# Experts' down weights: two neighbouring rows per partition, and transposes that read every second column

## The chip, the cores and the metric

The kernel runs on one core of a Trainium2 chip. The metric is the device time of one execution in microseconds (us), and what is compared is the median of several executions. The profile is one further execution, recorded by the hardware profiler.

A core has TensorE (PE in the rows; PEld is its load of the stationary operand), VectorE (DVE), ScalarE (ACT), GpSimd (POOL) and SyncE (SP), which here issues nearly all the transfers. Work buffers lie in SBUF on 128 partitions, the results of matrix products in the eight PSUM banks. Each product has a stationary operand, loaded by an LDWEIGHTS, and a moving one that streams past it. Transfers run on 16 DMA engines.

## The reference, cut to what matters

Two blocks follow one another on a sequence of 256 rows of width 1024, all in float32. The part that the change touches is the mixture of experts at the end of the first block: eight experts of inner width 3584, two of which are chosen for each row.

```python
def swiglu(h, w_gate, w_up, w_down):
    return (jax.nn.silu(h @ w_gate) * (h @ w_up)) @ w_down

def moe_swiglu(h, w_router, w_gate, w_up, w_down):
    ...
    for e in range(N_EXPERTS):
        y = swiglu(h, w_gate[e], w_up[e], w_down[e])
        out = out + gates[..., e:e + 1].astype(h.dtype) * y
    return out
```

`w_gate` and `w_up` are 1024x3584 for each expert, `w_down` is 3584x1024, so an expert has 42 MiB of weights and all eight have 336 MiB. Each row of `w_down` is 1024 float32, 4096 bytes in one run in HBM, and row r + 1 follows row r directly.

## The kernel before

Ahead of the experts come a gated linear attention, a dense feed-forward layer, an attention and the router; behind them a second block with its own mixers and feed-forward layer. The experts take the stretch from about 457 to 1440 us of the span.

**Pieces.** All weights come as pieces of 1 MiB, 2048 float32 on each of 128 partitions. For one expert, the inner width is cut into seven slices j of 512 (`EJ`). Each slice has six pieces: two of gate and two of up (`"g"`, `"u"`: 512 of the 1024 input rows by 512 columns, four rows on a partition in runs of 2048 bytes), and two of down (`"d"`: 256 of the 512 rows by all 1024 columns). The list `uorder` sets the order: gate and up of slice j, then down of slice j - 1. That makes 42 pieces for an expert (`UC`) and 336 for all eight, 112 of them down.

**Stations of a piece.** SP loads it (`load_expert`, L610 to 628) into one of six raw slots (`NRX`; four in `raw`, two in the arena, which is why rows name both). ACT writes a rounded copy of it (`wh`, L1027), DVE the difference between the piece and that copy (`wl`, L1543). PE then makes three products for each exact one (L1980 to 1982: both high parts, and each low part with the other's high part). There are four slots for `wh` and `wl` (`NW`). ACT waits for the transfer and for PE to be done with the piece four earlier; SP waits for DVE to be done with the piece six earlier.

**What PE does.** For each expert the rows that chose it are gathered by products with a one-hot matrix (L2299), 128 at a time. Then for each slice j: gate, then the transposes of slice j - 1 (`transposed`, L2327 to 2332), then up, then down of slice j - 1 (`down`; in the last slice `last_down`). Gate, up and down are 12 products a piece, 128x512 each. The activation `eact`, 128 rows by 512 inner columns in the arena, is transposed in four blocks of 128 columns into bank 4; ACT and DVE split the transposed blocks in two parts (`eactTh`, L1059; `eactTl`, L1622), and these are the stationary operands of down. Block k of the transposed activation, with inner columns on partitions, meets the rows of `w_down` that lie on the same partitions: block k in 0 and 1 goes with the first down piece, in 2 and 3 with the second.

**Which rows lie where.** The helper `kpn` puts rows k * 128 + p of a down piece at place k of partition p: each partition gets two runs of 4096 bytes that lie 512 KiB apart in HBM. So block k of the transposes is the 128 neighbouring columns from k * 128. In `T.transpose(out, in_, ident)` the data is the stationary operand and the identity the moving one; rows name the moving one first.

Each engine runs its own instructions in the order of the program text; nothing is scheduled by a planner here.

Of the kernel before, what the change touches and what calls it, by code (L numbers as in the profile page):

```python
# [16 lines left out]
def build(nc, IN, out):  # L17
# [6 lines left out]
    P = 128  # L24
    _, S, D = IN["x"].shape
# [35 lines left out]
    with ctx:  # L61
        def sb(name, shape, dt=F32):
            return ctx.enter_context(nc.sbuf_tensor(name, shape, dt))
# [3 lines left out]
        def sg(name):  # L67
            if name not in sems:
                sems[name] = ctx.enter_context(nc.semaphore(name))
            return sems[name]  # L70
# [18 lines left out]
        ident = sb("ident", [P, P])  # L89
# [22 lines left out]
        bank = [ctx.enter_context(nc.psum_tensor(f"bank{b}", [P, 512], F32)) for b in range(8)]  # L112
# [6 lines left out]
        def ar(n):  # L119
            a = arena[:, ar_at[0]:ar_at[0] + n]  # L120
            ar_at[0] += n
            assert ar_at[0] <= AR, ar_at[0]
            return a
# [194 lines left out]
        def kpn(ap):  # L318
            return ap.rearrange("(k p) n -> p k n", p=P)
# [141 lines left out]
        def moe_raw(c):  # L461

            s = c % NRX
            return (raw[:, (M0 + s) % NR, :] if s < NR else extra[:, s - NR, :]), raw_moe[s]
# [72 lines left out]
        eact = ar(2 * EJ).rearrange("p (a n) -> p a n", a=2)  # L537
# [65 lines left out]
        def _(sp):  # L603
# [11 lines left out]
            def load_expert(c, e):  # L615

                kind, j, k = uorder[c % UC]
                ee = e + c // UC
                to, arrived = moe_raw(c)
                if kind == "d":  # L620
                    r0 = j * EJ + k * (EJ // 2)
                    src = IN["moe_w_down"][0].rearrange("e f n -> (e f) n")[bass.ds(ee * FE + r0, EJ // 2), :]
                    src = kpn(src)
                else:
                    src = IN["moe_w_gate" if kind == "g" else "moe_w_up"][0, bass.ds(ee, 1), k * (D // 2):(k + 1) * (D // 2),
                                                                          j * EJ:(j + 1) * EJ]
                    src = src.rearrange("a (k p) n -> p (a k) n", p=P)
                sp.dma_start(to.rearrange("p (k n) -> p k n", k=src.shape[1]), src).then_inc(arrived, 16)
# [33 lines left out]
            for c in range(NR):  # L662
                split_done(sp, N_PRE - NR + c)
                load_expert(c, 0)
            for hp in range(SH // 2):
                see(sp, ("so", hp))
            for c in range(NR, NRX):
                load_expert(c, 0)
            sp.wait_ge(sg("more_ready"), 1)
            more = sp.value_load(more_i[0:1, 0:1], min_val=0, max_val=NPAIR)  # L670
            with sp.Fori(0, more + (NPAIR - 1)) as p:
                e = (p % NPAIR) * 2
                for c in range(NRX, PC):
                    moe_split(sp, lambda a, b: p * a + b, c - NRX)
                    load_expert(c, e)
                e2 = ((p + 1) % NPAIR) * 2
                for c in range(NRX):
                    moe_split(sp, lambda a, b: p * a + b, c + PC - NRX)
                    load_expert(c, e2)
# [1250 lines left out]
        def _(pe):  # L1930
            T = nc.tensor
# [170 lines left out]
            for k in range(KD):  # L2102
                ins = T.matmul(ps[0:GR, 0:S], wglr[:, k, :], xT[:, k, :], start=(k == 0), stop=(k == KD - 1))  # L2103
# [4 lines left out]
            for b in range(2):  # L2108
                ps = take(("gate", b))
                for j in range(2):  # L2110
                    hd = 2 * b + j
                    ins = T.matmul(ps[:, j * S:(j + 1) * S], wgu[:, hd * P:(hd + 1) * P], glrT, start=True, stop=True)
# [7 lines left out]
            for st in range(2):  # L2120
# [4 lines left out]
                for hd in range(GH):  # L2125
                    o = hd * S + st * P
                    ins = T.matmul(ps[0:GC, hd * P + GC:(hd + 1) * P], g["ke"][:, hd, st, :], g["qd"][:, o + GC:o + P],
                                   start=True, stop=True)
# [3 lines left out]
            for hd in range(GH):  # L2132
                o = hd * S
                ins = T.matmul(ps[:, hd * P:(hd + 1) * P], g["E"][:, o:o + P], g["B"][:, o + P:o + S], start=True, stop=True)
# [27 lines left out]
            for k in range(3):  # L2162
                n = V_ROWS[k]
# [87 lines left out]
            for hp in range(SH // 2):  # L2251
                ps = take(("so", hp))
                for i in range(2):
# [5 lines left out]
                    ins = T.matmul(ps[:, i * S + P:(i + 1) * S], sv[:, 1, vs], sU[:, hd, S:384], start=False, stop=True)  # L2259
# [50 lines left out]
            def experts(at, more_follow):  # L2310
# [5 lines left out]
                for i in range(2):  # L2316
# [10 lines left out]
                    def transposed(j):  # L2327
                        n = NEJ * i + j
                        pe.wait_ge(sg("moe_act"), at(2 * NEJ, n + 3))
                        for k in range(4):  # L2330
                            ins = T.transpose(bank[4][:, k * P:(k + 1) * P], eact[:, n % 2, k * P:(k + 1) * P], ident[:, :])  # L2331
                        ins.then_inc(sg("moe_Tfull"), 1)

                    def down(j, between=None):
# [37 lines left out]
                    for j in range(NEJ):  # L2372
                        n = NEJ * i + j
                        pe.wait_ge(sg("moe_act"), at(2 * NEJ, n + 1))
                        gate_up(bank[n % 2], "g", j)
                        if j == 1:
                            pe.wait_ge(sg("moe_h"), at(8, 4 * i + 1))
                        if j:
                            transposed(j - 1)
                        gate_up(bank[2 + n % 2], "u", j)  # L2380
                        if j == NEJ - 1:
                            down(j - 1, lambda: transposed(NEJ - 1))
                        elif j:
                            down(j - 1)
                        if j == 3:
                            pe.wait_ge(sg("moe_gates"), at(2, i + 1))
                            for t in range(TT):
                                T.transpose(bank[7][:, t * P:(t + 1) * P], oh[:, t, :], ident[:, :])
                            for t in range(TT):
                                ins = T.matmul(bank[7][:, S:S + 1], oh[:, t, :], gnow[:, t:t + 1], start=(t == 0), stop=(t == TT - 1))  # L2390
                            ins.then_inc(sg("moe_ohfull"), 1)
# [36 lines left out]
            for t in range(TT):  # L2428
                for k in range(KD):
                    ins = T.matmul(ps[:, 16 * t:16 * t + 16], xT[:, k, t * P:(t + 1) * P], ws[:, k, :],  # L2430
                                   start=(k == 0), stop=(k == KD - 1))
# [103 lines left out]
            for a, row in enumerate((mS, iF)):  # L2535
                for t in range(TT):
                    ins = T.transpose(ps[:, (TT * a + t) * P:(TT * a + t + 1) * P], row[:, t * P:(t + 1) * P], ident[:, :])
# [65 lines left out]
```

## Time and profile before

| what | value |
|---|---|
| median of 3 runs | 1820.54 us |
| lowest and highest | 1818.07 and 1821.10 us |
| the profiled execution, its own time | 1818.59 us |
| its span in the profile | 1816.9 us |
| PE busy | 1783.6 us (98%) |
| PEld, DVE, ACT, POOL busy | 85%, 77%, 62%, 6% |
[...]
| data moved | 479.27 MB in 244356 packets |

The profiled execution took 1818.59 us, of which 1816.9 are the span that the rows divide; 1.7 us lie around it. It is 1.95 us below the median of the three other runs. A busy PE says only that some product is under way: products are pipelined, one of 128x512 lasts some 390 ns from its start to its modelled end, but the next one starts earlier than that. The distance from start to start is therefore what a product costs.

### The profile page before, as it was taken

Reading aid. Unit: us, or ns where it says so; the run is one execution under the profiler, and the core shown is the slowest. Engines: PE = TensorE matmul, PEld = TensorE weight load, DVE = VectorE, ACT = ScalarE, POOL = GpSimd, SP = SyncE. Lnnn points to the kernel's source line nnn. Section 1 sums busy time; section 2 is a strip of 40 time slices with the busy share of each in tenths; the row PEclk is TensorE's granted clock in tenths of the full one; section 3 lists DMA queues with packets and bytes.
Section 4 is the critical chain, followed back from the end, with each engine's and each line's share of the span. In section 5 each row is a group of like instructions: output and inputs, shape, how many; then the busy total and the mean of one; then the engine's idle time right before and its main releaser. Section 6 shows DMA issues by size and latency. Waiting matters only on the chain.

```text
span 1816.9 us, 25802 instructions
## 1 busy us (share of the span) xinstructions
PE 1783.6 (98%) x10010; PEld 1542.8 (85%) x10010; DVE 1404.5 (77%) x1164; ACT 1131.6 (62%) x942; POOL 115.1 (6%) x133
## 2 busy tenths in 40 slices
PE   7999999999999999999999999999999999999999
PEld 6779999998888888888888888888888788789998
DVE  6565455656888988989889889888888879767775
ACT  6344344463677777776777767777767745745553
POOL 7000000000000000000000000000000008500000
PEclk9999999999999999999999999999999999999999
DMA  7445565542899998998998989989989944325561
GB/s 237 163 141 182 189 199 171 171 155 71 323 381 347 353 373 317 387 370 323 378 371 328 371 318 388 364 321 383 372 324 373 319 134 136 120 82 185 175 206 49
DMA packets 244356, 479.27 MB, mean 264 GB/s; under 512 B 11759, under 2 KB 80137, under 8 KB 244249
## 3 DMA queue, kind: packets, MB, share of 16 engines
q1 hardware_dynamic: 243385, 476.43, 73.3%
q8 instruction: 80, 1.31, 0.3%
q10 hardware_dynamic: 864, 1.31, 0.2%
q14 instruction: 27, 0.22, 0.0%
HBM read 476.66 MB, written 1.05 MB: 263 GB/s over the span
## 4 chain that ended last, share of the span: by engine, by line
PE 89%; DVE 7%; ACT 1%; issue 1%; DMA 0%; POOL 0%; DVEq 0%; ACTq 0%; SPq 0%; POOLq 0%
PE bank L1980 27%; PE bank L1982 27%; PE bank L1981 27%; DVE wl L438 2%; PE bank L2299 1%; PE bank L2331 1%; DVE xT L1296 1%; DVE xTl L1239 1%; PE bank L2368 0%; PE bank L1949 0%; PE bank L2369 0%; DVE h L1309 0%; DVE xn L1252 0%; PE bank L2103 0%; ACT xn L854 0%
## 5 line engine op out<-in xcount | busy, mean ns | idle before, releaser
L1980 PE MATMUL bank<-wh,xTh 128*128 128x512 f32 x1568 | 620.7, 396 | 4.3 <-DVE wl L438 2.8
L1982 PE MATMUL bank<-wh,xTl 128*128 128x512 f32 x1568 | 612.0, 390 | 0.0
L1981 PE MATMUL bank<-wl,xTh 128*128 128x512 f32 x1568 | 611.2, 390 | 0.0
L1543 DVE TENSOR_TENSOR wl<-raw,wh 128x2048 fp32r<-128x2048 f32 x224 | 512.2, 2291 | 92.6 <-ACT wh L1027 90.9
L1027 ACT ACTIVATE wh<-raw 128x2048 fp32r<-128x2048 f32 x224 | 429.2, 1918 | 120.7 <-PE bank L1982 120.7
L1980 PEld LDWEIGHTS bank<-wh,xTh 128*128 128x128 f32 x1568 | 295.2, 188 | 66.5 <-DVE wl L438 3.7
L1982 PEld LDWEIGHTS bank<-wh,xTl 128*128 128x128 f32 x1568 | 294.8, 188 | 62.7
L1981 PEld LDWEIGHTS bank<-wl,xTh 128*128 128x128 f32 x1568 | 295.3, 188 | 58.5
L438 DVE TENSOR_TENSOR wl<-raw,wh 128x2048 fp32r<-128x2048 f32 x112 | 254.7, 2292 | 68.3 <-ACT wh L431 66.5
L1980 PE MATMUL bank<-xTh,wh 128*128 128x256 f32 x1024 | 290.8, 284 | 1.2 <-DVE xTl L1239 0.8
L1981 PE MATMUL bank<-xTl,wh 128*128 128x256 f32 x1024 | 289.8, 283 | 0.0
L1982 PE MATMUL bank<-xTh,wl 128*128 128x256 f32 x1024 | 289.8, 283 | 0.0
L1543 DVE TENSOR_TENSOR wl<-arena,wh 128x2048 fp32r<-128x2048 f32 x112 | 255.6, 2286 | 0.4 <-ACT wh L1027 0.2
L1027 ACT ACTIVATE wh<-arena 128x2048 fp32r<-128x2048 f32 x112 | 215.3, 1922 | 52.0 <-PE bank L1982 52.0
L431 ACT ACTIVATE wh<-raw 128x2048 fp32r<-128x2048 f32 x116 | 219.5, 1912 | 39.4 <-PE bank L1982 32.5
L1980 PEld LDWEIGHTS bank<-xTh,wh 128*128 128x128 f32 x1024 | 196.4, 192 | 3.7 <-DVE xTl L1239 1.6
L1981 PEld LDWEIGHTS bank<-xTl,wh 128*128 128x128 f32 x1024 | 196.5, 192 | 0.7
L1982 PEld LDWEIGHTS bank<-xTh,wl 128*128 128x128 f32 x1024 | 196.4, 192 | 0.0
L1980 PE MATMUL bank<-wh,acth 128*128 128x512 f32 x192 | 75.3, 392 | 0.3 <-DVE actl L1493 0.3
L1981 PE MATMUL bank<-wl,acth 128*128 128x512 f32 x192 | 75.0, 390 | 0.0
L1982 PE MATMUL bank<-wh,actl 128*128 128x512 f32 x192 | 74.7, 389 | 0.0
L713 POOL TENSOR_TENSOR rstd<-ms,cst 128x4 f32<-128x4 f32 (+1 forms) x4 | 3.5, 865 | 1051.0 <-DVE ms L1683 1009.7
(379 smaller groups left out, 1384.6 us busy)
## 6 DMA issues: line engine op xcount, KB each, us to landing
raw<-in_moe_w_up SPq DMA_DIRECT2D x112, 1024.0 KB, 7.7
arena<-in_moe_w_gate SPq DMA_DIRECT2D x96, 1024.0 KB, 7.4
raw<-in_moe_w_down SPq DMA_DIRECT2D x96, 1024.0 KB, 7.2
raw<-in_w_up SPq DMA_DIRECT2D x22, 1024.0 KB, 5.5
raw<-in_moe_w_gate SPq DMA_DIRECT2D x16, 1024.0 KB, 7.5
arena<-in_moe_w_down SPq DMA_DIRECT2D x16, 1024.0 KB, 7.4
raw<-in_gla_w_in SPq DMA_DIRECT2D x12, 1024.0 KB, 7.8
raw<-in_w_in SPq DMA_DIRECT2D x12, 1024.0 KB, 6.3
```

The lines of the kernel that those rows point to most:

```text
L431: nc.scalar.activation(wh[:, i % NW, :], raw[:, i % NR, :], ACT.Copy).then_inc(hi_ready[ph], 1)
L438: V.tensor_tensor(wl[:, i % NW, :], raw[:, i % NR, :], wh[:, i % NW, :].bitcast(F32), ALU.subtract).then_inc(lo_of[i][0], 1)
L713: G(V.tensor_tensor(rstd[:, c0:c0 + n], ms[:, c0:c0 + n], c_half[:, 0:n], ALU.pow), "rstd_ready")
L1027: V.activation(wh[:, s, :], src, ACT.Copy).then_inc(sg("hi_moe"), 1)
L1239: C(V.tensor_tensor(hi_lo[1][ix], src[ix], hi_lo[0][ix].bitcast(F32), ALU.subtract), "xl_ready")
L1296: ins = V.tensor_tensor(dst[:, 4 * half:4 * half + 4, t * P:(t + 1) * P], ps, gains.unsqueeze(2).to_broadcast([P, 4, P]), ALU.mult)
L1543: V.tensor_tensor(wl[:, s, :], moe_raw(c)[0], wh[:, s, :].bitcast(F32), ALU.subtract).then_inc(lo_moe, 1)
L1980: T.matmul(o, xh, yh, start=first, stop=False)
L1981: T.matmul(o, xh, yl, start=False, stop=False)
L1982: return T.matmul(o, xl, yh, start=False, stop=last)
L2299: ins = T.matmul(b[:, k * P:(k + 1) * P], xn[:, t, kk * P:(kk + 1) * P], oh[:, t, :], start=(t == 0), stop=(t == TT - 1))
L2331: ins = T.transpose(bank[4][:, k * P:(k + 1) * P], eact[:, n % 2, k * P:(k + 1) * P], ident[:, :])
```

## The change

Two places change together. The transfer of a down piece puts rows 2p and 2p + 1 of the piece on partition p, so each partition gets one run of 8192 bytes and the whole piece is 1 MiB without a gap. The transposes take the columns to match: within each half of 256 columns, one block takes the even columns and the next the odd ones, so the stationary operand is read with a step of two elements (8 bytes). Sizes, counts, buffers, waits and the order of the work are as before. Every sum over inner columns has the same terms in another order.

```diff
@@ -620,7 +620,7 @@
                 if kind == "d":
                     r0 = j * EJ + k * (EJ // 2)
                     src = IN["moe_w_down"][0].rearrange("e f n -> (e f) n")[bass.ds(ee * FE + r0, EJ // 2), :]
-                    src = kpn(src)
+                    src = src.rearrange("(p k) n -> p k n", p=P)
                 else:
@@ -2328,7 +2328,8 @@
                         pe.wait_ge(sg("moe_act"), at(2 * NEJ, n + 3))
                         for k in range(4):
-                            ins = T.transpose(bank[4][:, k * P:(k + 1) * P], eact[:, n % 2, k * P:(k + 1) * P], ident[:, :])
+                            rows_of = eact[:, n % 2, k // 2 * S:(k // 2 + 1) * S].rearrange("p (f two) -> p two f", two=2)
+                            ins = T.transpose(bank[4][:, k * P:(k + 1) * P], rows_of[:, k % 2, :], ident[:, :])
```

No instruction is added, removed or moved on any engine. On SP's queue only the shape of the down transfers differs. Before, behind an up piece and ahead of the gate pieces of the next slice:

```order
L628 DMA raw<-in_moe_w_down 128x2x1024
L459 REGISTER_ALU
L628 ISA
L628 DMA raw<-in_moe_w_down 128x2x1024
L459 REGISTER_ALU
```

And in the changed kernel, at the same place:

```order
L628 DMA raw<-in_moe_w_down 128x2048
L459 REGISTER_ALU
L628 ISA
L628 DMA raw<-in_moe_w_down 128x2048
L459 REGISTER_ALU
```

Both are 1 MiB; the two runs of 1024 elements have become one of 2048.

## Rows read from the trace of the kernel before

**Rows 1.** Page: busy shares, clock by slices, packets, chain that ended last.

```profile
PE 1783.6 (98%) x10010; PEld 1542.8 (85%) x10010; DVE 1404.5 (77%) x1164; ACT 1131.6 (62%) x942; POOL 115.1 (6%) x133
...
PEclk9999999999999999999999999999999999999999
...
DMA packets 244356, 479.27 MB, mean 264 GB/s; under 512 B 11759, under 2 KB 80137, under 8 KB 244249
...
PE 89%; DVE 7%; ACT 1%; issue 1%; DMA 0%; POOL 0%; DVEq 0%; ACTq 0%; SPq 0%; POOLq 0%
```

**Rows 2.** Windows: busy us of PE, PEld, DVE, ACT, POOL; clock, DMA share, GB/s.

```profile
174.30:179.70 5.40, 5.40 (x26) 4.48 (x25) 5.07 (x5) 2.55 (x2) 0.00 (x0) 1.00 0.14 21
902.00:917.40 15.40, 15.40 (x69) 12.74 (x68) 13.86 (x12) 11.85 (x8) 0.00 (x0) 1.00 1.03 378
600.00:1400.00 800.00, 800.00 (x3729) 664.12 (x3728) 708.44 (x443) 585.76 (x399) 0.00 (x0) 1.00 0.97 358
```

**Rows 3.** Waits of PE, 460 to 1445 us: who, for whom, total, times, longest.

```profile
PE bank L1980 <- DVE xTl L1590: 0.7, 1, 0.7
```

**Rows 4.** Line L2331, the transposes: durations ns min/median/max.

```profile
L2331 PEld LDWEIGHTS bank<-ident,arena x224: 139/141/143, 477.9 to 1439.1; 128*128 128x128 f32 x112
L2331 PE MATMUL bank<-ident,arena x224: 270/272/273, 478.2 to 1439.2; 128*128 128x128 f32 x112
```

**Rows 5.** Chain around a group of transposes: start, us on the chain.

```profile
901.02 0.44 PE bank L2331 x4
```

**Rows 6.** Timeline of PE in the experts, slice of 900 to 918 us.

```profile
900.86 0.60 PE L2331 MATMUL bank<-ident,arena 128*128 128x128 f32 x4
901.21 0.47 PE L1980 MATMUL bank<-wh,xTh 128*128 128x512 f32 x1
901.52 0.39 PE L1981 MATMUL bank<-wl,xTh 128*128 128x512 f32 x1
...
917.64 0.60 PE L2331 MATMUL bank<-ident,arena 128*128 128x128 f32 x4
```

**Rows 7.** ACT, exponentials over pieces of a tile: the line, and its first instruction.

```profile
L865 ACT ACTIVATE arena<-arena x8: 417/418/447, 1499.1 to 1553.3; 128x256 f32<-128x256 f32 x8
...
1499.09 0.45 ACT L865 ACTIVATE arena<-arena 128x256 f32<-128x256 f32 x1 [0.18 <-DVE arena L1750]
```

**Rows 8.** Timeline of DVE, products of tiles: step of two, then runs of two, four.

```profile
1501.30 1.09 DVE L1322 TENSOR_TENSOR arena<-arena 128x256 f32<-128x256 f32 x1
1511.05 0.42 DVE L1322 TENSOR_TENSOR arena<-arena 128x256 f32<-128x256 f32 x1
1515.84 0.97 DVE L1322 TENSOR_TENSOR arena<-arena 128x256 f32<-128x256 f32 x1
```

**Rows 9.** DMA view: transfers by source, KB each, median us from issue to landing.

```profile
raw<-in_moe_w_up SPq DMA_DIRECT2D x112, 1024.0 KB, 7.7
...
raw<-in_moe_w_down SPq DMA_DIRECT2D x96, 1024.0 KB, 7.2
...
raw<-in_ffn_w_gate SPq DMA_DIRECT2D x11, 1024.0 KB, 5.4
...
raw<-in_ffn_w_down SPq DMA_DIRECT2D x11, 1024.0 KB, 5.0
```

**Rows 10.** The down transfers of the experts: us from issue to landing.

```profile
DMA to landing us min/median/max: 4.8/7.2/9.3
```

**Rows 11.** Timelines of SP and ACT: a down piece issued, and read.

```profile
902.76 0.37 SPq L628 DMA_DIRECT2D raw<-in_moe_w_down  x1
...
915.12 1.92 ACT L1027 ACTIVATE wh<-raw 128x2048 fp32r<-128x2048 f32 x1 [0.80 <-PE bank L1982]
```

**Rows 12.** Timeline of PE in the feed-forward layer: two products, 22 steps apart.

```profile
174.51 0.40 PE L1981 MATMUL bank<-wl,acth 128*128 128x512 f32 x1
...
179.51 0.39 PE L1982 MATMUL bank<-wh,actl 128*128 128x512 f32 x1
```

**Rows 13.** Waits of SP's queue, whole run: for whom, total, times, longest.

```profile
SPq L628 <- DVE wl L1543: 779.0, 328, 7.2
```

## The prediction, made blind

> **What bounds the kernel now.** I read the page first, then the windows, then PE's own waits. On the page PE is busy for 98% of the span, its clock row stands at full speed in every slice, and the chain that ended last lies on PE for 89% and on DMA for 0% [rows 1]. In the windows (the three are feed-forward down products, one slice of the experts, and most of the experts) the experts are denser than that: between 600 and 1400 us PE is busy for 800.00 of 800.00 us at a granted clock of 1.00, while the DMA share is 0.97 at 358 GB/s [rows 2]. Both look full, so the waits must tell which one sets the pace. In the whole stretch of the experts PE waited 0.7 us, once, for DVE [rows 3]; no wait of PE or ACT there ends on a DMA. SP, by contrast, stood 779.0 us in 328 waits for DVE to give back a slot [rows 13]. The transfers follow the compute, and PE's instruction stream sets the end.
>
> So a change counts here if it changes what PE's own instructions cost, or if it makes a transfer so late that its slack is used up.
>
> **Part one, the transfers.** 112 down pieces of 1 MiB change from two runs of 4096 bytes per partition to one of 8192. Follow one piece. SP issues it at 902.76, and ACT, whose sixth copy since the freed slot's it is, reads it at 915.12, held back by PE and not by the transfer [rows 11]. That is 12.36 us from issue to use. The down transfers take 7.2 us in the median and 9.3 at most [rows 10]: 5.2 us of slack, 3.1 in the worst case. This slack, ahead of ACT's copy, is the cover.
>
> How does run length act on landing? Up pieces with runs of 2048 bytes land in 7.7 us, down pieces with runs of 4096 in 7.2; in the feed-forward layer gate pieces with runs of 1024 take 5.4 and down pieces with 4096 take 5.0 [rows 9]. Longer runs gain 0.4 to 0.5 us, in other places of the queue, too. I expect 7.2 to fall by 0 to 0.5 us. Since nothing waits for it, the saving only makes SP's pieces lie ready earlier. I cost it at nothing; an increase would be nothing too until it reaches 3.1 us in the worst piece.
>
> Could lighter transfers speed up PE itself, through less traffic into the buffers that PE reads? The trace has the comparison. In the feed-forward layer, at a DMA share of 0.14 and 21 GB/s [rows 2], 22 steps from product to product take 179.51 - 174.51 = 5.00 us, 0.2273 each [rows 12]. In the experts, at 1.03 and 378 GB/s [rows 2], the 72 products of one slice lie between 901.21 and the next transposes at 917.64; the 71 steps from 901.52 take 16.12 us, 0.2270 each [rows 6]. With eighteen times the traffic a product costs the same. I take 0.
>
> **Part two, the transposes.** There are 8 experts x 7 slices x 4 = 224, all of whose stationary loads now step by two. A group starts at 900.86, the next product at 901.21, and the one after that at 901.52, where the usual step would be 0.227: the group costs 0.35 + 0.31 - 0.227 = 0.433 us [rows 6], and the chain gives 0.44 [rows 5]. Four transposes, 0.109 each; 56 groups make 24.5 us of PE time. Nothing hides that time: what a transpose gains or loses is gained or lost at the end of the kernel. The load is part of it, and its 139 to 143 ns [rows 4] are longer than the 109 ns between transposes, so loads and transposes run into one another with no gap to spare.
>
> The trace of before shows no TensorE load with a step. I bound it from both sides.
> - Below: 0. The step doesn't change the number of elements or instructions, and no row shows a strided read that is faster than a plain one; a gain is excluded on that ground.
> - Nearest row above: ScalarE's exponentials read and write 256 float32 in pieces of a tile. In the first one the pieces are single elements with a step of two, in the later ones runs of 2 to 128. The first took 447 ns, the median is 418 [rows 7]. That is 29 ns for 256 elements with both sides strided; for 128 elements 14.5 ns, times 224: 3.2 us.
> - Far row: VectorE's product of tiles took 1.09 us with a step of two, 0.42 with runs of two, but 0.97 with runs of four [rows 8]. An instruction without the step is as slow, so most of it is something else, and I give no weight to the factor of 2.6. Taken at its word it is 1.6 x 24.5 = 39 us.
>
> I take 0, the lower end: the closest row loses 7% with a strided read and a strided write together, the load has only the read, and that instruction was the first of its kind, so part of its 29 ns may be start-up. Both ends stay for the range.
>
> On strided reads the row above shows +29 ns. [...] Nothing in this trace shows where TensorE's own limit lies.
>
> What stands behind the transposes: the first down product of a slice comes a whole up stage later, some 5.4 us (24 products x 0.227), and needs ACT's and DVE's parts of bank 4. A few tenths more on the transposes would be hidden there. Only PE's own time counts.
>
> **The sum.** Profiled execution 1818.6 us + transfers 0 + PE's steps 0 + transposes 0 = 1818.6. That execution lies 1.95 us below the median of the three runs, so the forecast for the median is **1820.5 us**, with its own range 1817 to 1824.
>
> **Rivals.**
> - **The strided load takes twice as long.** Mechanism: a load that takes every second element gets half as many useful elements from each read of the buffer. Place: the 224 stationary loads. Price: 0.109 us more for each, 24.5 us, giving 1845 us. It decides from 16 ns per transpose (3.6 us in all). For it: loads and transposes are back to back, nothing covers them, and ScalarE's row is not zero. Against it: at +7% ScalarE is far from double. A mild form, 16 to 30 ns per transpose, gives 1824 to 1827.
> - **Longer runs relieve PE.** If the products of the experts (336 pieces x 12 = 4032) each got 1 ns shorter, 4.0 us would be gained: 1816.5 us. For it: DMA share 0.97. Against it: 0.2273 and 0.2270 us a step at 21 and at 378 GB/s.
> - **The transfers become the bound.** A slice takes 917.64 - 900.86 = 16.78 us [rows 6] for six pieces, 2.80 each. If each down piece occupied the engines 2.8 us longer, the slice would grow by up to 5.6 us, and 56 slices by 313. It decides when landing rises from 7.2 beyond 12.4 us. For it: there is little idle DMA time. Against it: the direction of the landing times above.
> - **The change does nothing.** If the 8192 bytes are cut into two packets of 4096, the packet count stays at 244356 [rows 1] and the time is that of the forecast.
>
> **How the numbers follow.** A measurement of this kernel tells about 0.2%, 3.6 us, from no change. Forecast (the rival that does nothing included) 0.75; PE relieved 0.06; mild penalty 0.06; doubled load 0.11; transfers as the bound 0.02. The range has to hold the forecast's 1817 to 1824, and reaches down to 1816.5 less half a microsecond and up to the mild penalty's 1827: 1816 to 1827 leaves out the last two, 0.13. Faster 0.06, same 0.75, slower 0.19.
>
> **What would show it.** The line of the transposes should keep its loads near 141 ns and its matmuls near 272, and a group should stand on the chain with 0.44 us; a doubled load shows as about 0.87. The steps of the 128x512 products should stay at 0.227. The packets should fall by 112 x 128 = 14336 if each run is one packet. Down pieces should land in 6.7 to 7.2 us, SP should still wait for DVE, and PE for no transfer. The prediction is wrong if the group has grown beyond 0.50 us (16 ns x 4), or if a wait that ends on a DMA appears in the experts.

## The result, and the profile after

The changed kernel took 1822.99 us in the median of 18 runs (1821.42 to 1826.3), the kernel before 1820.40 (1814.96 to 1823.34). The ratio is 1.0021, with a 95% interval of 1.0014 to 1.0027: a small slowdown, 2.5 to 4.9 us, clear of noise. The profiled execution took 1822.76 us; its span is 1821.0 at a mean granted clock of 0.997, against 1816.9 at 0.998 before.

First the page, where little has moved. The packets fell by 14336 (230020 from the 244356 of [rows 1]), exactly 112 x 128, so each run of 8192 bytes is one packet, and the down pieces land sooner: 7.0 us in the median and 8.5 at most, from 7.2 and 9.3 [rows 10].

```profile
span 1821.0 us, 25802 instructions
...
DMA packets 230020, 479.27 MB, mean 263 GB/s; under 512 B 11759, under 2 KB 80137, under 8 KB 215577
...
PE 89%; DVE 7%; ACT 1%; issue 1%; DMA 0%; POOL 0%; DVEq 0%; ACTq 0%; SPq 0%; POOLq 0%
```

```profile
DMA to landing us min/median/max: 4.7/7.0/8.5
```

The line of the transposes (now L2332) is where the change shows; it answers to [rows 4]. The columns are minimum, median and maximum in ns.

```profile
L2332 PEld LDWEIGHTS bank<-ident,arena x224: 194/199/205, 477.6 to 1441.6; 128*128 128x128 f32 x112
L2332 PE MATMUL bank<-ident,arena x224: 271/280/282, 477.8 to 1441.7; 128*128 128x128 f32 x112
```

A load with a step of two lasts 199 ns in the median instead of 141, a transpose 280 instead of 272. The chain gives a group 0.46 us, where [rows 5] has 0.44, and PE's timeline shows the same slice as [rows 6], from one group to the next:

```profile
901.75 0.62 PE L2332 MATMUL bank<-ident,arena 128*128 128x128 f32 x4
902.13 0.47 PE L1980 MATMUL bank<-wh,xTh 128*128 128x512 f32 x1
902.44 0.39 PE L1981 MATMUL bank<-wl,xTh 128*128 128x512 f32 x1
...
918.59 0.62 PE L2332 MATMUL bank<-ident,arena 128*128 128x128 f32 x4
```

From group to group it is 918.59 - 901.75 = 16.84 us, where it was 917.64 - 900.86 = 16.78. One such pair is at the limit of the timeline's two decimals, so I took the mean over the 32 slices of a run that have 72 products and nothing else between two groups (24 in `same_delay`, which changes eight of them). In the four kernels with plain single transposes there (before, `load_only`, `permute_on_dve`, `same_delay`) it agrees within 0.001 us:

| kernel | last product to group | group to next product | next but one to the twelfth, each | slice |
|---|---|---|---|---|
| before | 0.231 | 0.353 | 0.2289 | 16.787 |
| after | 0.240 | 0.380 | 0.2308 | 16.840 |

Further behind, a product's step is 0.2267 in both. So a slice grew by 0.053 us: 0.009 ahead of the group, 0.027 in it, and some 0.02 over the ten products behind it. 56 groups make 3.0 us, 13.3 ns for each of the 224 transposes. The experts as a whole, from the first group to the last, grew from 960.67 to 963.54 us, by 2.9.

The spans of the two profiled executions differ by 4.1 us. Of that 2.9 lie in the experts, -0.4 ahead of them, and 1.6 behind, where the program did not change. There the windows show TensorE's granted clock, at the place where the second block begins (columns as in [rows 2]); first the changed kernel, then the kernel before at the same place in the program:

```profile
1474.50:1477.90 3.40, 3.40 (x30) 3.32 (x29) 1.06 (x3) 2.76 (x2) 0.00 (x0) 0.97 1.10 369
1477.90:1481.30 3.40, 3.40 (x16) 3.40 (x17) 0.86 (x5) 0.95 (x1) 1.16 (x1) 0.50 0.46 142
1481.30:1484.70 3.40, 3.40 (x18) 3.40 (x18) 0.00 (x0) 0.00 (x0) 0.00 (x0) 0.53 0.00 0
```

```profile
1475.40:1478.80 3.40, 3.40 (x30) 3.40 (x31) 0.86 (x5) 0.89 (x1) 1.17 (x1) 1.00 0.44 136
```

In the changed kernel's profile the clock stood at 0.50 of full for nearly 7 us, from 1477.7 to 1484.5, and PE got through 16 to 18 products in 3.4 us where it otherwise does 30. Counted product by product, it lost 3.0 us there against the kernel before. The timeline shows what PE did as it fell, 32 products of only 16 columns:

```profile
1474.88 4.30 PE L2431 MATMUL bank<-ws,xT 128*128 128x16 f32 x32
```

In the profile of before, the clock stood at 1.00 there, behind the same 32 products. In that profile it fell later, from 1590.5 to 1597.3 us. The changed kernel's clock fell a second time at nearly that place, for half as long. First the kernel before, then the changed one:

```profile
1590.50:1597.30 6.80, 6.33 (x18) 5.26 (x19) 5.67 (x17) 4.00 (x6) 0.00 (x0) 0.50 0.01 2
```

```profile
1597.10:1600.50 3.40, 3.40 (x11) 2.73 (x11) 2.99 (x13) 2.56 (x4) 0.00 (x0) 0.51 0.02 5
```

In the profile of `load_only`, below, the clock stayed up at both places, and against it the two stretches of these rows cost 3.0 and 1.6 us. So the 1.6 us behind the experts are 3.0 lost at 1480 less 1.4 that the changed kernel lost less at 1600. That the clock can fall at these places is no property of the change: the experiments have it without the step and without the new transfers (0.50 from 1499.4 us in `twice_plain`, from 1594.1 in `same_delay`).

### The profile page after: what moved, and what is told of

Same layout as the page of the kernel before. It is cut to its first block, busy times and chain, and to the rows that moved or that the text cites. A ratio compares the mean times of both kernels' runs of the same rounds, so it can differ in the third digit from the quotient of the medians.

```text
span 1821.0 us, 25802 instructions
## 1 busy us (share of the span) xinstructions
PE 1788.1 (98%) x10010; PEld 1549.8 (85%) x10010; DVE 1404.5 (77%) x1164; ACT 1131.7 (62%) x942; POOL 114.8 (6%) x133
## 2 busy tenths in 40 slices
DMA packets 230020, 479.27 MB, mean 263 GB/s; under 512 B 11759, under 2 KB 80137, under 8 KB 215577
## 4 chain that ended last, share of the span: by engine, by line
PE 89%; DVE 7%; ACT 1%; issue 1%; DMA 0%; POOL 0%; DVEq 0%; ACTq 0%; SPq 0%; POOLq 0%
PE bank L1980 27%; PE bank L1982 27%; PE bank L1981 27%; DVE wl L438 2%; PE bank L2299 1%; PE bank L2332 1%; DVE xT L1296 1%; DVE xTl L1239 1%; PE bank L2369 0%; PE bank L1949 0%; PE bank L2370 0%; DVE h L1309 0%; DVE xn L1252 0%; PE bank L2103 0%; ACT xn L854 0%
```

## The experiments

Three questions were open. Is it the transfers or the step that costs? Does the tail belong to it? And what does a strided operand cost TensorE, in a load that stands bare, in one that is hidden, and on the moving side?

**Transfers alone.** `load_only` is the kernel before with the first half of the diff.

```diff
-                    src = kpn(src)
+                    src = src.rearrange("(p k) n -> p k n", p=P)
```

> The kernel before with only the transfers changed (8192 bytes in one run per partition); the transposes read neighbouring columns as before, so the down products pair activations with the wrong rows of the weights, and the output is not the reference's. Theory of the step (the 224 stationary loads with a step of two cost 13 to 14 ns each, 0.054 us a group): nothing is left here, slice of the experts 16.79 us as before, ratio 0.999 to 1.001. Rival, the transfers' new shape costs the time (by buffer traffic beside PE): slice 16.84 us, ratio 1.0015 to 1.003.

Measured: 1818.07 us against 1818.74, ratio 0.9994 (0.9985 to 1.0003); the mean slice is 16.787 us. The timeline has 900.64 to 917.42:

```profile
900.64 0.60 PE L2331 MATMUL bank<-ident,arena 128*128 128x128 f32 x4
...
917.42 0.60 PE L2331 MATMUL bank<-ident,arena 128*128 128x128 f32 x4
```

The new transfers cost nothing and bring nothing (16.787 us a slice with both).

**The step alone.** `step2_only` is the second half of the diff, with the old transfers.

```diff
-    ins = T.transpose(bank[4][:, k * P:(k + 1) * P], eact[:, n % 2, k * P:(k + 1) * P], ident[:, :])
+    rows_of = eact[:, n % 2, k // 2 * S:(k // 2 + 1) * S].rearrange("p (f two) -> p two f", two=2)
+    ins = T.transpose(bank[4][:, k * P:(k + 1) * P], rows_of[:, k % 2, :], ident[:, :])
```

> The kernel before with only the transposes changed (step of two), the transfers as before; again activations meet the wrong rows, so the output is not the reference's. Theory of the step: slice 16.84 us, loads of the transposes near 199 ns, 3.0 us over the experts, ratio 1.0013 to 1.0027. Rival, transfers' shape: slice 16.79 us, ratio 0.999 to 1.001.

Measured: 1823.02 us, ratio 1.0020 (1.0011 to 1.0029), mean slice 16.840 us; group to next product 0.380, ten products behind at 0.2307. The whole effect is there, number by number.

```profile
900.64 0.62 PE L2332 MATMUL bank<-ident,arena 128*128 128x128 f32 x4
...
917.48 0.62 PE L2332 MATMUL bank<-ident,arena 128*128 128x128 f32 x4
```

**New transfers without the step on PE.** In `permute_on_dve` VectorE does the reordering.

```diff
+    def by_two(a):
+        return a.rearrange("p (h f two) -> p h two f", h=2, two=2)
-    V.tensor_tensor(eact[:, n % 2, :], esg[:, n % 2, :], bank[2 + n % 2][:, :],
+    V.tensor_tensor(eact[:, n % 2, :].rearrange("p (h two f) -> p h two f", h=2, two=2),
+                    by_two(esg[:, n % 2, :]), by_two(bank[2 + n % 2][:, :]),
                     ALU.mult).then_inc(sg("moe_act"), 1)
```

> The new transfers, but VectorE's product that makes the activation (L1640) reads its two sources with a step of two and stores even and odd columns in blocks, so that the transposes read neighbouring columns; the output is the reference's. Theory of the step: slice back at 16.79 us, loads 141 ns, ratio 0.999 to 1.001, provided VectorE's product, 0.68 us before, stays under some 3 us. Rival, transfers' shape: slice 16.84 us. If VectorE's product grows so much that PE waits, a wait of PE on L1622 or L1543 shows.

Measured: 1820.18 us, ratio 0.9999 (0.9990 to 1.0008), mean slice 16.787 us. VectorE's product reads two sources with a step of two, one in SBUF and one in PSUM, in 681 ns (first row); in the kernel before it is L1640 with 682 (second row).

```profile
L1642 DVE TENSOR_TENSOR arena<-arena,bank x56: 679/681/683, 475.8 to 1437.9; 128x512 f32<-128x512 f32 x56
```

```profile
L1640 DVE TENSOR_TENSOR arena<-arena,bank x56: 678/682/683, 475.7 to 1437.8; 128x512 f32<-128x512 f32 x56
```

This undoes the loss, but it is no faster than the kernel before: there is nothing to win from the transfers. It also answers the far row of the prediction. VectorE's product of tiles in [rows 8] took 1.09 us with a step of two, but here the step costs VectorE nothing (681 ns against 682); what made that row so long is not shown.

**A delay of the same size without a step.** In `same_delay` the four plain transposes of slice 2 are done twice for each expert. In the changed kernel's profile the tail was 1.6 us longer, and the clock was at 0.50 of full near 1480 us. If the tail depends on when the stretch behind the experts begins, a delay alone may lengthen it by 1 to 3 us, a ratio of 1.002 to 1.004.

```diff
-                            ins = T.transpose(bank[4]...
+                            for twice in range(2 if j == 2 else 1):
+                                ins = T.transpose(bank[4]...
```

> The kernel before, with the four plain transposes of one slice of each expert (j = 2) done twice: 32 more transposes of 0.109 us, 3.5 us more in the experts and no step anywhere. [...] Rival, the lower clock comes with the step or the transfers: tail as before, 377.8 us from the last transposes to the end, ratio 1.0017 to 1.0021.

Measured: 1822.12 us, ratio 1.0022 (1.0012 to 1.0031), which holds the delay alone (3.5 us, 1.0019) as well as the delay with a somewhat longer tail. The profile has the delay alone: the experts grew by 3.5 us, to 964.18, and from the last group to the end it is 378.1 us, where the kernel before has 378.0. The clock was down for 6.8 us at the same place of the program in both (from 1594.1 us here, from 1590.5 before). Runs at the same mean clock agree roughly. At 0.998 this kernel took 1821.77 us in the mean of 5 runs, the kernel before on that chip 1817.59 in 14, which is 4.2 us more. At 1.000 it took 1818.68 in one run, and `load_only` 1815.25 in two: 3.4 us.

The place of the lower clock moves between profiles of kernels that cost the same. In the profile of `load_only` the clock stayed up until the very last stage, and its span is 1813.6 us, the shortest of all. In that of `permute_on_dve` it was down at 1475 to 1482 us and again near 1595, and its span is 1818.5; its tail is 379.67 us, that of the changed kernel 379.69. In that of `twice_plain`, below, which has neither the step nor the new transfers, it fell at the same place of the program, at 1499.4 us, behind the start of the same 32 products. That is why the runs of one kernel scatter over 5 us and more, and the 1.6 us in the tail of the changed kernel's profile are this scatter.

How often it happens is another matter. All 18 runs of the changed kernel had a mean clock of 0.993 to 0.997. On the chip of these four experiments 14 of 33 runs of the kernel before reached 0.998, 6 of 11 of `load_only` and 4 of 11 of `permute_on_dve`, but only 1 of 11 of `step2_only`. This is a hint that the step makes the lower clock more frequent, and it would explain why `step2_only`'s ratio stands for 3.6 us where its experts grew by 2.9. No run here was made to show it.

**Steps of three and four.** One line of the kernel before changes (4 and 509 in place of 3 and 382 for a step of four).

```diff
-    eact[:, n % 2, k * P:(k + 1) * P]
+    eact[:, n % 2, k:k + 382:3]
```

> The kernel before with transposes that read every third column (12 bytes from element to element); the transfers as before, so the output is not the reference's. With a step of one a load lasts 141 ns and a slice of the experts 16.787 us, with two 199 ns and 16.840. Theory that a load costs by how many bytes it passes over: some 215 to 260 ns, slice 16.86 to 16.90. [...]

> [...] Theory by bytes: load 230 to 320 ns, slice 16.88 to 16.95. [...]

Measured for three: ratio 1.0001 (0.9991 to 1.0011), mean slice 16.813 us. For four: 1.0003 (0.9993 to 1.0014), slice 16.814. The loads, step three and then step four:

```profile
L2331 PEld LDWEIGHTS bank<-ident,arena x224: 192/198/200, 477.7 to 1440.3; 128*128 128x128 f32 x112
```

```profile
L2331 PEld LDWEIGHTS bank<-ident,arena x224: 197/204/213, 477.8 to 1440.4; 128*128 128x128 f32 x112
```

The theory by bytes missed, in the loads (198 and 204 ns) and in the slices. Each of the three steps adds 57 to 63 ns to the load's row, but the wider ones, 12 and 16 bytes, cost less in time, 0.027 us a slice where two costs 0.053. A cost of 0.027 us a slice is 1.5 us in all, too little for the ratios to tell from nothing; it is read from the traces alone. In the parts: with three, group to next product is 0.370 us and the products behind are undisturbed (0.2291); with four it is 0.390, dearer than with two, but the ten products behind run at 0.2277. Why the products behind the group feel a step of two and not the wider ones is open.

**The step on hidden loads.** `hidden_step2` interleaves the two halves of the tile that holds the experts' stationary operands.

```diff
-        xgh, xgl = xTh[:, :, 0:P], xTl[:, :, 0:P]
-        eactTh, eactTl = xTh[:, :, P:S], xTl[:, :, P:S]
+        xTh2, xTl2 = (a.rearrange("p k (s two) -> p k s two", two=2) for a in (xTh, xTl))
+        xgh, xgl = xTh2[:, :, :, 0], xTl2[:, :, :, 0]
+        eactTh, eactTl = xTh2[:, :, :, 1], xTl2[:, :, :, 1]
```

> The kernel before, but all stationary operands of the experts' gate, up and down products (4032 loads) lie with a step of two: gathered input and transposed activation share a tile element by element instead of half by half. Transposes and transfers as before; the output is the reference's. Theory that a strided load costs only where nothing hides it: each of these loads is issued one product ahead and has 0.227 us, so the step of the products stays 0.227, ratio 0.999 to 1.001 (loads in the rows 188 to some 245 ns). Rival, a strided load costs some 13 ns wherever it stands: 4032 x 13 = 52 us, ratio 1.028. ScalarE and VectorE now store with a step, which may lengthen L1059 and L1622 but has slack.

Measured: 1842.40 us, ratio 1.0128 (1.0111 to 1.0145), so 23 us for 4032 loads, 5.8 ns each. No wait was added; the products themselves step by 3.50 / 15 = 0.233 us instead of 0.227:

```profile
900.05 0.39 PE L1981 MATMUL bank<-wh,xTh 128*128 128x512 f32 x1
...
903.55 0.39 PE L1981 MATMUL bank<-wh,xTh 128*128 128x512 f32 x1
```

Theory and rival both missed. A strided load that is issued a product ahead, 0.233 us, is not free here; it costs 5.8 ns, about half of the 13.3 in a transpose. Its row is 193 ns where it was 188, so here the row grew by about what the load costs.

ScalarE and VectorE store these operands with a step in this run. Their stores lie in a small part of each slice, while the products step by 0.233 us all through it, so I put the price down to the reads. ScalarE's own instruction shows what such a store costs it, with a source that has no step: 637 ns where it was 594 (first this run, then the kernel before). VectorE's took 684 ns in both.

```profile
L1060 ACT ACTIVATE xTh<-bank x56: 629/637/647, 479.4 to 1462.2; 128x512 fp32r<-128x512 f32 x56
```

```profile
L1059 ACT ACTIVATE xTh<-bank x56: 591/594/600, 478.9 to 1439.5; 128x512 fp32r<-128x512 f32 x56
```

**The step on the moving side.** `moving_step2` reads `wh` and `wl` of the gate and up pieces with a step of two.

```diff
+    h2, l2 = (w_.rearrange("p (a k) n -> p a (k n)", k=2)[:, k // 2, :].rearrange("p (n two) -> p two n", two=2)[:, k % 2, :]
+              for w_ in (h_, l_))
-    ins = mm3(b[:, :], xgh[:, kk, :], xgl[:, kk, :], h_[:, k, :], l_[:, k, :], kk == 0, kk == KD - 1)
+    ins = mm3(b[:, :], xgh[:, kk, :], xgl[:, kk, :], h2, l2, kk == 0, kk == KD - 1)
```

> The kernel before, but the moving operands of the gate and up products (2688 of 4032) are read with a step of two; the weights lie as before, so the output is not the reference's. [...] Rival, the moving operand is slowed too (half as many useful bytes per read): up to twice 0.227 us, 2688 x 0.227 = 610 us, ratio up to 1.33.

Measured: 2422.86 us, ratio 1.332 (1.3294 to 1.3347), 603 us for 2688 products, 0.224 each. The timeline has 1002.80 - 1000.08 = 2.72 us for six steps, 0.453 us instead of 0.227:

```profile
1000.08 0.63 PE L1982 MATMUL bank<-wh,xTl 128*128 128x512 f32 x1
...
1002.80 0.63 PE L1982 MATMUL bank<-wh,xTl 128*128 128x512 f32 x1
```

Here the doubling that was feared for the load is real: 0.453 is twice 0.227. That it comes from fewer useful elements in each read of the buffer is argued, not shown.

**A further transpose, plain and strided.** `twice_plain` and `twice_step2` do each transpose of their kernel twice (`for twice in range(2):` ahead of `T.transpose`).

> The kernel before with each of the 224 transposes done twice in a row; the output is the reference's. It prices a further plain transpose in a full row. All theories: 0.107 to 0.110 us each, 24.0 to 24.6 us more in all, ratio 1.013 to 1.014.

> The changed kernel with each of its 224 transposes done twice in a row; the output is the reference's. Theory of the half rate: with a step the load reads one element where it read two, so it takes some 53 ns longer (141 to 199 ns in the rows, the same for steps of 2, 3 and 4), but a transpose of float32 already takes 0.109 us, about as long as the doubled load, so a further one costs little more than a plain one, 0.107 to 0.113 us; the extra of a group lies at its edges and in the products around it. Rival, each strided load costs its 13 ns for itself: 0.122 us for a further one, 27.4 us for all 224.

Measured: ratio 1.0136 (1.0102 to 1.0170) and 1.0161 (1.0121 to 1.0201), two runs each, so the ratios can't tell the two apart and the traces have to. Plain, then strided, start of the group and the next product:

```profile
911.42 1.03 PE L2332 MATMUL bank<-ident,arena 128*128 128x128 f32 x8
912.21 0.48 PE L1980 MATMUL bank<-wh,xTh 128*128 128x512 f32 x1
```

```profile
913.79 1.10 PE L2333 MATMUL bank<-ident,arena 128*128 128x128 f32 x8
914.65 0.47 PE L1980 MATMUL bank<-wh,xTh 128*128 128x512 f32 x1
```

The means over the run are 0.790 and 0.860 us for eight, 0.353 and 0.380 for four. A further plain transpose costs 0.109 us, a further strided one 0.120: 11 ns for the step inside the row. Most of the price belongs to each load, as the rival said (it had 13); the rest of the 13.3 lies at the edges of a group and in the products behind it.

**Short products in the rounded format.** Eight extra products of 128 columns, plain and with a strided stationary operand (`0:2 * P:2` in place of `0:P`).

```diff
+    if kind == "g" and half and j >= 2:
+        for extra_k in range(8):
+            ins = T.matmul(bank[4][:, 0:P], h_[:, extra_k % 4, 0:P], h_[:, extra_k % 4, S:S + P],
+                           start=True, stop=True)
```

> The kernel before with eight extra products of 128x128 by 128x128 in the rounded format (fp32r) behind the gate products of slices 2 to 6 of each expert, 40 groups, 320 products, operands taken from the weights in SBUF, results overwritten by the transposes that follow; the output is the reference's. [...] Both theories: 0.055 to 0.110 us each (no row before shows one); this run is the base of the next.

The strided run was to test the theory of the half rate, which would put a strided load at 0.107 us. If plain products got below 0.07 us, such a load would stand bare behind them, and a product would cost at least 0.04 us more.

> The same eight extra products, but their stationary operand is read with a step of two (every second of 256 columns). [...] Rival, a stepped load costs 6 to 13 ns as in the transposes and in the hidden loads: 0.01 us more.

```profile
914.00 1.00 PE L2327 MATMUL bank<-wh 128*128 128x128 f32 x8
914.84 0.62 PE L2335 MATMUL bank<-ident,arena 128*128 128x128 f32 x4
```

```profile
916.90 1.05 PE L2327 MATMUL bank<-wh 128*128 128x128 f32 x8
917.79 0.62 PE L2335 MATMUL bank<-ident,arena 128*128 128x128 f32 x4
```

Each kernel ran once (1855.46 and 1858.58 us), so only the traces are compared. As means over all 40 groups: 0.840 us plain and 0.888 strided, that is 0.105 and 0.111 a product, 6 ns for the step. The test did not reach what it was made for. It asked for plain products below 0.07 us, and they took 0.105. The lower end of the expectation, 0.055 us, no run shows. The 0.105 is about what the theory of the half rate gives a strided load (0.107; this figure and the 53 ns behind it are the theory's own and shown by no run, the load's row grew by 58), so 0.111 doesn't exclude that theory. What stands against it is the further transpose above, 0.120 us where it had 0.107 to 0.113, and the hidden loads, which cost 6 ns each behind products of 0.227 us. Whether a strided load itself runs at half rate, and whether it reads one element where a plain one reads two, stays open; the 58 ns in the row of the transposes were not its price in any run. A product of 128 columns takes 0.105 us in this format, a transpose of float32 0.109, though a product of 512 takes only 0.227.

## Why the prediction was wrong

**What bounds the kernel: right.** PE's instruction stream sets the end. Every gain and loss inside the experts is one of PE's own steps, and no wait of PE there is new: it is one, of 0.7 or 0.8 us, in every trace.

**The transfers: right, with their size.** They cost 0 (`load_only`, 0.9994). Landing fell by 0.2 us where 0 to 0.5 was forecast, and the packets fell by exactly 112 x 128. The argument that traffic doesn't slow PE, from 0.2273 and 0.2270 us a product at 21 and 378 GB/s, had no run of its own; a product's step stayed at 0.2267 us with the new transfers.

**The transposes: the step that failed.** The term "transposes 0" of the sum measured 3.0 us. The mechanism was named and the place was right (224 loads that nothing hides). The mistake was the choice between the bounds: "I take 0, the lower end", with two reasons, that ScalarE's instruction also stores with a step and that its 29 ns may contain start-up. (The group's own sum is off a little, without effect: 56 times 0.433 is 24.2 us, not 24.5.)

The second reason was wrong, and the trace of before had the row for it. The second exponential, right behind the first and with the same step of two, took 0.45 us as well, so it was no start-up. (The fourth, with runs of two elements, still took 0.43.)

```profile
1499.57 0.45 ACT L866 ACTIVATE arena<-arena 128x256 f32<-128x256 f32 x1
```

The first reason was right in itself, as `hidden_step2` shows: a store with a step alone lengthened ScalarE's 512 elements by 43 ns. Taken to 256 elements, as an estimate, that is some 21 of the 29 ns; 8 are left for the read, 4 for a load of 128 elements, 0.9 us over 224. But it is a reason for less than 3.2 us, not for 0, which no row supported.

Taken whole, the row gives 14.5 ns a load and a forecast of 1823.7 us; the load cost 13.3 and 1823.0 was measured. By the estimate above this closeness is luck: most of the row's 29 ns is the store, which a load of TensorE doesn't have.

**The rivals.** The doubled load fell as a price (0.109 us feared, 0.0133 measured); what doubled in a run is the step of a product whose moving operand is strided (0.453 us for 0.227). The mild form, 16 to 30 ns, began just above the truth. Between the forecast's 0 and those 16 ns no case was named; only the forecast's own range, 1817 to 1824, kept open to the row's 3.2 us, held the 13.3 ns that were measured. "Longer runs relieve PE" and "the transfers become the bound" fell with `load_only`. The packet count, 14336 lower, rules out that the 8192 bytes were cut in two.

**The signs to look for.** "A group beyond 0.50 us" was too coarse a mark: it was tied to 0.2% of the kernel, and the group came to 0.46 us, while means over a trace repeat within 0.001 us. The loads "near 141 ns" were the better sign, and it failed at once (199 ns), though their row overstates the price.

## What to carry to other kernels

A stationary operand of float32 that is read with a step of two cost 5.8 ns a load here where the load was hidden, and 13.3 in the transposes; that is nothing in one product and was 1.3% of a kernel with 4032 of them. A moving operand with a step of two took twice the time here (0.453 us for 0.227), so if a layout must be undone, let VectorE do it in an instruction that runs anyway (681 ns against 682), or put the step on the stationary side. And where the nearest row of a trace gives a price for an operation that PE can't hide, zero needs evidence of its own; a reason why the row may be too high is a reason for a lower price or a wider range. First look for the row that tests the reason.

## What the runs showed of the hardware

- The duration of a load in its row was a poor measure of its price in the transposes: 141 to 199 ns, +58, cost 11 to 13 ns of time; in the hidden loads 188 to 193, +5, cost about 6.
- Products of 128x512 stepped by 0.227 us, with a strided stationary operand by 0.233, with a strided moving operand by 0.453.
- VectorE read SBUF and PSUM with a step of two at no cost (681 and 682 ns), unlike TensorE, and in `hidden_step2` stored with one at no cost (684 ns). ScalarE's store of 512 elements with a step of two took 43 ns more (637 and 594).
- The granted clock fell to 0.50 of full at one to four places behind the experts (two in the profile of before, two in that of after, one in `load_only`'s, four in `step2_only`'s), and runs of one kernel follow it: on one chip the kernel before took 1817.6 us in the mean at a clock of 0.998 and 1820.3 at 0.995. Two kernels that differ by 3 us are best told apart by the mean step of the same group in their traces.
